# Attention units by key/value head: four query heads of one head pair with 512-column value products, in place of two heads of each with paired score products

## The reference

```
s = einsum('bcqkgd,bcjkd->bckgqj', q, k) * scale + bias      # masked to the window
m = max(max(s), sink);  p = exp(s - m)
o = einsum('bckgqj,bcjkd->bcqkgd', p / (sum(p) + exp(sink - m)), v)
```

## Time and profile before

| | |
|---|---|
| time, median of 3 runs | 3380.55 us (3378.43 to 3385.72) |
| the profiled execution | 3380.55 us, of which 3377.9 us between first and last instruction |
| PE busy | 3242.9 us (96%) |
| DVE, ACT, POOL busy | 1550.0 (46%), 1061.8 (31%), 476.1 us (14%) |
| mean granted TensorE clock | 0.983 of full speed |
| read from and written to HBM | 481.13 and 139.44 MB |

### The profile page before, as it was taken

The page is one execution under the profiler, slowest core; times in us unless marked ns, Lnnn a source line. Parts: engine busy times, 40 slices in busy tenths (PEclk is TensorE's granted clock), DMA queues, the critical chain, the costliest instruction groups (busy, mean ns, idle before and its releaser), DMA issues.

```text
span 3377.9 us, 43935 instructions
## 1 busy us (share of the span) xinstructions
PE 3242.9 (96%) x17526; PEld 2753.6 (82%) x17526; DVE 1550.0 (46%) x2779; ACT 1061.8 (31%) x1924; POOL 476.1 (14%) x515
## 2 busy tenths in 40 slices
PE   7999989999999999999999999999999998999997
PEld 5777768878787878888787888888798997899985
DVE  6977745545775640013594542003395555200012
ACT  3656432234345420003254421003143532200021
POOL 2840000000470000000281000000074000100000
PEclk9999989999999999999999999999999999999998
DMA  7854467777543355555553354555554233455443
GB/s 233 281 213 179 168 243 290 285 279 285 210 167 137 113 200 178 194 195 195 200 195 127 125 187 165 194 189 201 199 176 140 102 111 106 142 175 175 169 150 107
DMA packets 177898, 623.35 MB, mean 185 GB/s; under 512 B 20592, under 2 KB 28080, under 8 KB 177184
## 3 DMA queue, kind: packets, MB, share of 16 engines
q1 hardware_dynamic: 176736, 620.15, 52.4%
q10 hardware_dynamic: 960, 0.40, 0.0%
HBM read 481.13 MB, written 139.44 MB: 184 GB/s over the span
## 4 chain that ended last, share of the span: by engine, by line
PE 79%; DVE 3%; ACT 2%; DMA 1%; issue 1%; POOL 0%; SPq 0%; DVEq 0%; ACTq 0%; POOLq 0%
PE PS L747 50%; PE PS L801 7%; PE PS L803 7%; PE PS L802 6%; PE PS L783 2%; PE PS L876 2%; PE PS L865 1%; PE PS L924 1%; PE PS L895 1%; PE PS L896 1%; PE PS L897 1%; PE PS L731 1%; PE PS L914 1%; DVE x L1444 1%; DVE PS L1439 1%
## 5 line engine op out<-in xcount | busy, mean ns | idle before, releaser
L747 PE MATMUL PS<-h_hi,w_hi 128*128 128x512 f32 (+1 forms) x3288 | 1053.4, 353 | 24.7 <-DVE u L1602 15.4
L747 PE MATMUL PS<-h_hi,w_lo 128*128 128x512 f32 (+1 forms) x3288 | 1053.7, 353 | 0.0
L747 PE MATMUL PS<-h_lo,w_hi 128*128 128x512 f32 (+1 forms) x3288 | 1044.2, 350 | 0.0
L747 PEld LDWEIGHTS PS<-h_hi,w_hi 128*128 128x128 f32 x3288 | 579.5, 189 | 108.0 <-issue 20.7
L747 PEld LDWEIGHTS PS<-h_lo,w_hi 128*128 128x128 f32 x3288 | 579.3, 189 | 90.0 <-issue 1.7
L747 PEld LDWEIGHTS PS<-h_hi,w_lo 128*128 128x128 f32 x3288 | 579.5, 189 | 81.3
L692 POOL TENSOR_TENSOR y<-y,prod 128x512 f32<-128x512 f32 (+1 forms) x333 | 407.8, 1251 | 231.2 <-ACT prod L1158 220.4
L1392 DVE SCALAR_TENSOR_TENSOR PS<-u,dw,PS 128x512 f32<-128x512 f32 (+1 forms) x604 | 434.0, 765 | 7.0
L1753 DVE TENSOR_TENSOR f<-PS,tmp 128x512 f32<-128x512 f32 (+1 forms) x88 | 61.5, 699 | 670.6 <-PE PS L747 651.9
L801 PE MATMUL PS<-w_hi,f_hi 128*128 128x512 f32 x748 | 297.3, 398 | 5.8 <-DVE f L1753 5.4
L803 PE MATMUL PS<-w_hi,f_lo 128*128 128x512 f32 x748 | 295.3, 395 | 0.0
(11 more groups left out here) (185 smaller groups left out, 3919.1 us busy)
## 6 DMA issues: line engine op xcount, KB each, us to landing
w_lo<-lo_dram SPq DMA_DIRECT2D x372, 512.0 KB, 4.4
w_hi<-hi_dram SPq DMA_DIRECT2D x372, 512.0 KB, 3.5
w_raw<-in_w_stream SPq DMA_DIRECT2D x124, 512.0 KB, 3.9
hi_dram<-w_hi SPq DMA_DIRECT2D x124, 512.0 KB, 4.0
lo_dram<-w_lo SPq DMA_DIRECT2D x124, 512.0 KB, 3.9
x<-in_x_prompt SPq DMA_DIRECT2D x4, 2048.0 KB, 10.8
out_y_prompt<-x SPq DMA_DIRECT2D x4, 2048.0 KB, 7.1
xs<-in_x_prompt SPq DMA_DIRECT2D x12, 512.0 KB, 5.5
```

Source lines behind the costliest of these rows:

```text
L747: last = nc.tensor.matmul(PS[:, k0 + off, 0:n], w, x[:, k, c0:c0 + n], start=first and k == 0, stop=stop and k == KT - 1)
```

## The change

`unit(n)`'s last number, `n % 2`, is now read as `kv`: a unit takes all four query heads of one k/v head, and its partner in the pair takes those of the other. Three functions follow from it. `scores` contracts all its matmuls over the same 64 partitions `d`, head by head. `times_values` takes one value slice per key tile and streams all 512 columns of `pt_hi` or `pt_lo`; both units of a pair add into the whole bank, where before each filled its own half. `score_max` reads bias and sink of the four heads of one k/v head, and the sink sum needs no rearranged access.

```diff
--- before.py
+++ after.py
@@ -843,27 +843,24 @@
                 last.then_inc(w_used, 1)
 
             def scores(b, n):
-
-                _, tt, hp = unit(n)
+                _, tt, kv = unit(n)
+                d = slice(HD * kv, HD * kv + HD)
                 gu = U0[b] + n
-                if hp == 0:
+                if kv == 0:
                     pe.wait_ge(qs_lo_ok, gu // 2 + 1)
                 if gu:
                     pe.wait_ge(ttr_done, 4 * gu)
-                if tt < 4:
-                    parts = [(0, 2 * P, k_hi[:, tt * P:tt * P + 2 * P], k_lo[:, tt * P:tt * P + 2 * P])]
-                else:
-                    parts = [(0, P, ck_hi[:], ck_lo[:]),
-                             (P, P, k_hi[:, P + WIN0:P + TX], k_lo[:, P + WIN0:P + TX])]
-                for hx in range(2):
-                    for c0, cn, khi, klo in parts:
-                        for qx, kx, start, stop in ((qs_hi, khi, True, False), (qs_hi, klo, False, False),
-                                                    (qs_lo, khi, False, True)):
-                            for kv in range(2):
-                                d = slice(HD * kv, HD * kv + HD)
-                                out = PS[:, 2 + kv, hx * 2 * P + c0:hx * 2 * P + c0 + cn]
-                                last = nc.tensor.matmul(out, qx[d, 2 * hp + hx, :], kx[d, :],
-                                                        start=start, stop=stop)
+                for h in range(4):
+                    out = PS[:, 2 + h // 2, (h % 2) * 2 * P:(h % 2 + 1) * 2 * P]
+                    if tt < 4:
+                        parts = [(out, k_hi[d, tt * P:tt * P + 2 * P], k_lo[d, tt * P:tt * P + 2 * P])]
+                    else:
+                        parts = [(out[:, 0:P], ck_hi[d, :], ck_lo[d, :]),
+                                 (out[:, P:2 * P], k_hi[d, P + WIN0:P + TX], k_lo[d, P + WIN0:P + TX])]
+                    for o, khi, klo in parts:
+                        nc.tensor.matmul(o, qs_hi[d, h, :], khi, start=True, stop=False)
+                        nc.tensor.matmul(o, qs_hi[d, h, :], klo, start=False, stop=False)
+                        last = nc.tensor.matmul(o, qs_lo[d, h, :], khi, start=False, stop=True)
                 last.then_inc(qk_done, 1)
 
             def transpose_probs(b, n):
@@ -879,22 +876,21 @@
 
             def times_values(b, n):
 
-                _, tt, hp = unit(n)
+                _, tt, kv = unit(n)
                 gu = U0[b] + n
                 o = gu // 2
                 pe.wait_ge(pt_lo_ok, gu + 1)
-                if hp == 0 and o >= 2:
+                if kv == 0 and o >= 2:
                     pe.wait_ge(o_out, o - 1)
                 for kt in range(2):
                     vt = (6, 5)[kt] if tt == 4 else tt + kt
-                    out = PS[:, 6 + o % 2, hp * 2 * P:(hp + 1) * 2 * P]
-                    for kv in range(2):
-                        vh, vl = (v[:, vt, :, :].rearrange("p a d -> p (a d)")[:, kv * HD:kv * HD + P]
-                                  for v in (v_hi, v_lo))
-                        ph, pl = (px[:, kt, kv * 2 * P:(kv + 1) * 2 * P] for px in (pt_hi, pt_lo))
-                        nc.tensor.matmul(out, vh, ph, start=kv == 0 and kt == 0, stop=False)
-                        nc.tensor.matmul(out, vh, pl, start=False, stop=False)
-                        last = nc.tensor.matmul(out, vl, ph, start=False, stop=kv == 1 and kt == 1)
+                    vh, vl = (v[:, vt, :, :].rearrange("p a d -> p (a d)")[:, kv * HD:kv * HD + P]
+                              for v in (v_hi, v_lo))
+                    out = PS[:, 6 + o % 2, :]
+                    nc.tensor.matmul(out, vh, pt_hi[:, kt, :], start=kv == 0 and kt == 0, stop=False)
+                    nc.tensor.matmul(out, vh, pt_lo[:, kt, :], start=False, stop=False)
+                    last = nc.tensor.matmul(out, vl, pt_hi[:, kt, :], start=False,
+                                            stop=kv == 1 and kt == 1)
                 last.then_inc(pv_done, 1)
 
             def mean_bank(b):
@@ -1454,21 +1450,20 @@
 
             def score_max(b, n):
 
-                gu, (hh, _, hp) = U0[b] + n, unit(n)
+                gu, (hh, _, kv) = U0[b] + n, unit(n)
                 dve.wait_ge(qk_done, gu + 1)
                 if gu:
                     dve.wait_ge(pt_done, gu)
                 for h in range(4):
-                    head = KT * (h // 2) + 4 * hh + 2 * hp + h % 2
+                    head = KT * kv + 4 * hh + h
                     nc.vector.tensor_tensor_reduce(
                         out=p[:, h, :], in0=PS[:, 2 + h // 2, (h % 2) * 2 * P:(h % 2 + 1) * 2 * P],
                         in1=bias[:, head, :], scale=1.0, scalar=sink_sb[:, head:head + 1],
                         op0=ALU.add, op1=ALU.max, accum_out=mx[:, h:h + 1]).then_inc(ttr_done, 1)
                 dve.wait_ge(ttr_done, 4 * gu + 4)
                 link(nc.vector.tensor_scalar(nmx, mx, -1.0, None, ALU.mult))
-                sinks = sink_sb[:].rearrange("p (k h) -> p k h", k=2)[:, :, 4 * hh + 2 * hp:4 * hh + 2 * hp + 2]
-                TT(es_in.rearrange("p (k h) -> p k h", k=2), sinks, nmx.rearrange("p (k h) -> p k h", k=2),
-                   ALU.add).then_inc(mx_ok, 1)
+                head = KT * kv + 4 * hh
+                TT(es_in, sink_sb[:, head:head + 4], nmx, ALU.add).then_inc(mx_ok, 1)
 
             def probs_lo(b, n):
                 gu = U0[b] + n
```

## The result

The changed kernel takes 3421.99 us (median of 4 runs, 3419.22 to 3426.93) where the kernel before takes 3380.62 us beside it: a ratio of 1.0121, 95% interval 1.0108 to 1.0134. That is 41.4 us slower. Forecast were 3425.5 us, and 45.0 us more. The profiled execution has a span of 3420.8 us, 42.9 us more than before.

A forecast was written before the change was run, and what follows sets the result against it. TensorE was taken as the bound through attention. Terms 45.1 + 0.6 + 5.4 - 1.3 - 4.1 - 0.7 = +45.0 us on 3380.55 gave 3425.5 us, 1.3% slower, own range 3419 to 3431 (87%).

The forecast's parts named there:

- TensorE is the bound, and steps are its price: Attention: TensorE is the bound almost everywhere, so the change is priced by start-to-start distance of its instructions.
- Scores: 64 units of 256 key columns: twelve lone steps of 0.1175 us replace six in twos, 0.705 us a unit, 45.1 us.
- Both rivals on the step: Weight loads exposed, 0.22 us a step, 3494 us, 6%; lone matmul costs half a two, 0.059 us, 3376.4 us, 3%.
- the twos: Score rows before: two matmuls per 0.1175 us step, read as both array halves working at the same time.
- Sample units: Four units of sample frames: twelve more score steps of 0.112 us, 1.34 us each, 5.4 us; one hidden, -1.3 us.
- The clock behind unit 16: Value products behind unit 16's wait: a shorter wait might keep the clock up, saving up to 1.1 us; counted as nothing.
- The value products: Six 512-column steps of 0.23 us replace twelve of 0.12: 0.06 us less a unit, -4.1 us over 68 units.
- Into waits: Blocks 1 and 2, first unit's transposes waiting for exponentials: 0.36 us used up in each, -0.7 us over two blocks.
- Block 0: Its first unit's scores run at half clock, 0.215 us a step: 0.6 us more.
- the rival that it hides its share: Block 0: if VectorE's lateness sets the pace, sixteen units' 11 us vanish, 3414 us; chance 4%.
- the 0.6 us wait for `qs_lo`: Block 0: TensorE waits once, 0.6 us, for `qs_lo`; counted among the waits that don't shrink.
- the stated range: 3419 to 3431 us: value-product bounds, clock behind unit 16, and 0.003 us on a score step, given as 1.3 us.

The follow-up runs named there:

- The doubled scores: All score matmuls made twice: on the kernel before 3423.64 us (ratio 1.012), on the kernel after 3544.51 us (ratio 1.048).
- the serial order: Kernel before with the k/v loop of scores outermost, six matmuls on one half of the partitions, then six on the other: 3413.74 us, ratio 1.0096.
- fives order: Kernel before with score matmuls in blocks of five on one half of the partitions, five on the other, then one and one: 3396.2 us, ratio 1.0052.
- the second run: Profiled execution of the unchanged kernel after in one experiment set: the four attention stretches sum to 647.0 us, the rest 2781.4 us.
- the third: Profiled execution of the unchanged kernel after in another experiment set: the four attention stretches sum to 638.5 us, the rest 2779.8 us.
- the cut of the value products: Kernel after with ten of the twelve 512-column value products of each pair of units cut into 256 columns: 3424.75 us, ratio 1.0127.
- three sets: The kernel after, unchanged, measured beside the kernel before three times: 3421.99 us (ratio 1.0121), 3425.46 us (1.0134) and 3420.48 us (1.0119).
- orders by four, five and six: Kernel before with score matmuls in blocks of four, five or six on one half of the partitions, then the other: 3378.77, 3396.2 and 3413.74 us.
- the scores doubled in twos: Kernel before with all its score matmuls made twice, order otherwise kept: 3423.64 us, ratio 1.012.

## Why the prediction was right

- **TensorE is the bound, and steps are its price.** It held. A steady unit grew by 9.55 - 8.89 = 0.66 us; 0.645 were forecast (0.705 less 0.06). The doubled scores gave the same price a second time.
- **Scores.** 0.1175 us a lone step was taken, 0.117 measured, and the group went to 1.60 us (1.61 said). Both rivals on the step are out: neither 0.06 nor 0.22 occurs after the start of a group at full clock. The Trainium skill (TensorE: Matmul & The Clock Gate, section The mechanism) says that weight loads overlap running matmuls only where row groups differ; here twelve loads in a row go to one row group, and the ten steps behind the first are still as short as in twos, so the measurement decides against that sentence. The same section of the Trainium skill has matmuls start strictly in order; the serial and the fives order above show a start ahead of three older ones.
- **What in the working was right for too narrow a reason.** I read the twos as neighbours in order that share their time. They are two queues, as it were, with a reach of four. The prediction didn't suffer, since after the change no matmul of the other half is within reach at all.
- **Sample units.** 2.8 us forecast, 2.82 measured in each of the four (0.112 a step) in this execution. Their first one went into the wait as said (3.08 to 1.64 us).
- **The clock behind unit 16.** I left it out and kept 1.1 us for the range. At that place the clock did stay full, but it fell some 3.6 us after unit 17's scores began. Units 16 to 17 took 15.3 us where 16.65 were before, and 17 to 18 took 15.05 for 12.24, 1.5 more than its scores explain. So in this execution the cost was moved, not saved. The other two differ: 17 to 18 took 18.13 us in the second run, where the clock fell just before unit 17's scores and they took 5.31 us, and 13.49 in the third, where it stayed up. The term changes from one execution to the next, and leaving it to the range was right.
- **The value products.** -0.06 us a unit, as the steps of 0.120 and 0.23 show in the trace. As a time this term, 4 us, can't be told by these runs. The Trainium skill's overhead of about 60 cycles (TensorEngine Tiling (Array Packing), section Instruction Overhead) would have made it an estimated 10 us; the cut of the value products shows 0.01 us a matmul where that asks for 0.025.
- **Into waits.** Block 1's second unit, whose transposes waited, shows 0.21 us ahead of them now; the 0.36 us are used up. Blocks 1 and 2 grew by 9.5 us each for 9.3 forecast (15 x 0.645 less 0.36).
- **Block 0** grew by 10.5 us for 10.3 forecast, so the rival that it hides its share is out. But two errors cancel here. Its first unit grew by 2.1 us, from 9.08 to 11.17, where the steps and the half clock asked for 1.3; over 256 to 270 us the mean granted clock is 0.63 where it was 0.76. And the 0.6 us wait for `qs_lo`, which the working had among the waits that don't shrink, is gone: that unit took 9.58 us before and 9.60 after.
- **Block 3** grew by 14.7 us where the steps ask for 12.8. There TensorE's clock is at half for 3.4 us in the first unit:

```profile
2674.00:2684.00 10.00, 9.80 (x63) 9.53 (x64) 5.29 (x19) 6.98 (x16) 0.00 (x0) 0.83 0.30 107
```

With the four last units' scores beyond the table (3 x 0.65 + 1.3), attention cost 47.4 us in this execution; the rest of the kernel, which the change doesn't touch, took 4.5 us less. That their sum of 42.9 comes near 45.0 is partly luck. In the three profiled executions of the kernel after the rest moves by 3 us and the last block by 6, so the 45.0 forecast and 41.4, 44.4 and 39.2 us measured in three sets agree as well as the runs can tell.

One size in the stated range is off: 0.003 us on a score step moves all twelve lone steps of 64 units, which is 2.3 us and not 1.3. It changes neither the sum nor a chance.

## What to carry to other kernels

Where a contraction fills only half of the partitions, the two halves behaved like two machines here: what counts is the longer of the two lists of matmuls, and a layout that puts one head group in a unit by itself idles the other half. They needn't alternate one by one, but in these runs the partner had to stand within four places to run without loss. Before trading that for wider matmuls, price both in start-to-start steps: here a merge of two 256-column products gave 0.01 us a matmul, the loss of a partner 0.1175 us.

## What the runs showed of the hardware

- A score matmul started before older ones that wait for the other half of the array, up to four places ahead and no further (orders by four, five and six). Only score matmuls of this kernel were tried, each with a weight load of its own; whether the four counts matmuls or their loads too isn't shown.
- The first step of a score group costs 0.22 us instead of 0.12 with 256 columns (0.16 instead of 0.112 with 128). In the serial order the second half shows it too when its own matmuls begin (315.35 to 315.57), and so it does by fives. Why isn't shown.
- With new weights each time, 128 columns cost 0.112 us over 64 rows and 0.111 over 128, 256 columns 0.117 over 64 rows and 0.120 over 128, and 512 columns 0.23 over 128 rows.
- The granted clock fell to half without any wait of TensorE. In the kernel after with doubled scores, a unit's 48 lone score matmuls of 128 columns began at 2980.50 us at full clock and from 2983.4 on stood 0.213 us apart:

```profile
2983.12 0.27 PE L863 MATMUL PS<-k_hi,qs_lo 64*128 64x128 f32 x1
...
2983.54 0.42 PE L863 MATMUL PS<-ck_hi,qs_lo 64*128 64x128 f32 x1
2983.76 0.41 PE L861 MATMUL PS<-k_hi,qs_hi 64*128 64x128 f32 x1
```

What the clock judges by was not tried. That narrow matmuls on half of the rows preceded this fall is what the trace shows. Within attention it stayed down for long only in the last block, where the weight steps too bring narrow matmuls (32 columns beside 512). Near unit 17 the clock fell in the other kernels as well: with the scores doubled in twos it was down from unit 17's first scores on, which began 1.7 us behind a wait of 1.85 us. So lone matmuls aren't the only thing that can stand ahead of a fall.
